# Conv rows stored per weight tile, the sample delta rule by heads, and a later start of the first two delta chunks

## The reference, cut to what matters

```python
h = rmsnorm(x, norm_g)
proj = jnp.einsum('bld,de->ble', h, w_in)
x_ext = jnp.concatenate([conv_prefix, qkv_raw], axis=1)
qkv = causal_short_conv(x_ext, conv_w)          # 4 taps, then SiLU
new_conv = x_ext[:, -(CONV_W - 1):]
o_a, s_new = gated_delta_rule(qa, ka, va, g, beta, s0)       # 4 heads of 128
# per chunk: solve (I + A) against v and k, then
#   v_new = u_c - w_c S ;  o_c = q_c S + attn v_new ;  S = S * gl + k_c^T v_new
o_a = rmsnorm(o_a, dn_norm_g) * silu(z_a)
o_b = merge_dilations(parts) * silu(z_b)        # 8 heads of 64, windows (128,1) (512,4) (2048,16)
y = x + einsum('ble,ed->bld', concatenate([o_a, o_b]), w_out)
y_prompt, y_sample = rmsnorm(yp, final_norm_g), rmsnorm(ys, final_norm_g)
```

## Time and profile before

| | us |
|---|---|
| median of three runs | 1985.62 (1980.72 to 1986.15) |
| the profiled execution | 1983.66 |
| its span in the profile | 1982.0 |
| PE busy in the span | 1726.9 (87%) |

### The profile page before, as it was taken

One profiled execution on the slowest core, in us unless ns is written; L12 is line 12 of the kernel. 1 busy time (PEld: TensorE's weight loads), 2 busy tenths in 40 slices (PEclk: granted clock), 3 DMA queues, 4 the chain that ended last, 5 costly groups with the idle time before them and its releaser, 6 DMA issues. The chain is left out here.

```text
span 1982.0 us, 27674 instructions
## 1 busy us (share of the span) xinstructions
PE 1726.9 (87%) x9674; PEld 1430.6 (72%) x9674; DVE 821.0 (41%) x1890; ACT 639.3 (32%) x1547; POOL 355.2 (18%) x367
## 2 busy tenths in 40 slices
PE   5999999999999998908677898898899559889897
PEld 5998888888888886706577788788788427666674
DVE  3535213511521350154744444444443346445462
ACT  4433212311421230111322443443345214333342
POOL 0000000000000000016023412421422333233231
PEclk9999999999999999958888998898898659999999
DMA  5424586676568679799355547446422456664660
GB/s 173 126 70 156 173 225 170 161 202 225 145 201 204 177 155 127 226 208 280 117 107 147 127 112 181 108 106 171 117 60 70 119 162 197 192 201 154 176 191 32
DMA packets 250186, 309.69 MB, mean 156 GB/s; under 512 B 69244, under 2 KB 198780, under 8 KB 240588
## 3 DMA queue, kind: packets, MB, share of 16 engines
q1 hardware_dynamic: 250068, 308.14, 58.3%
HBM read 228.50 MB, written 146.44 MB: 189 GB/s over the span
## 5 line engine op out<-in xcount | busy, mean ns | idle before, releaser
L326 PE MATMUL pj<-hT_hi,w_hi 128*128 128x512 f32 x896 | 360.1, 402 | 1.8 <-DVE raw L571 1.8
L328 PE MATMUL pj<-hT_hi,w_lo 128*128 128x512 f32 x896 | 352.6, 393 | 0.0
L327 PE MATMUL pj<-hT_lo,w_hi 128*128 128x512 f32 x896 | 352.3, 393 | 0.0
L328 PEld LDWEIGHTS pj<-hT_hi,w_lo 128*128 128x128 f32 x896 | 168.7, 188 | 38.4
L326 PEld LDWEIGHTS pj<-hT_hi,w_hi 128*128 128x128 f32 x896 | 169.0, 189 | 37.0 <-issue 2.1
L327 PEld LDWEIGHTS pj<-hT_lo,w_hi 128*128 128x128 f32 x896 | 169.1, 189 | 34.6
L1477 PE MATMUL o_ps<-pt,vt 128*65 128x256 f32 (+3 forms) x560 | 152.2, 399 | 4.3 <-DVE ot L1699 2.2
L678 POOL IOTA row_at<- 128x1 int32 x1 | 0.1, 139 | 843.3 <-POOLq L2507 843.3
L1541 ACT ACTIVATE pt<-pt_ps 128x512 f32<-128x512 f32 x144 | 84.8, 589 | 157.8 <-PE pt_ps L1455 157.4
L2233 PE MATMUL y_bank<-wo_hi,mh 128*128 128x512 f32 (+1 forms) x272 | 113.2, 416 | 6.8 <-POOL ml L2218 4.6
L533 DVE SCALAR_TENSOR_TENSOR acc<-raw,conv_wt,acc 128x512 f32<-128x512 f32 x144 | 108.3, 752 | 5.1
(11 more groups left out here) (452 smaller groups left out, 3507.3 us busy)
## 6 DMA issues: line engine op xcount, KB each, us to landing
out_dram<-in_cache_k_win_dram SPq DMA_DIRECT2D x56, 584.0 KB, 7.5
out_dram<-in_cache_v_win_dram SPq DMA_DIRECT2D x56, 584.0 KB, 7.0
w_raw<-in_w_in_dram SPq DMA_DIRECT2D x31, 512.0 KB, 10.5
qk_ch<-sil SPq DMA_DIRECT2D x32, 256.0 KB, 3.1
z_ch<-xr SPq DMA_DIRECT2D x32, 256.0 KB, 4.2
wqk<-hi SPq DMA_DIRECT2D x32, 256.0 KB, 5.3
wqk<-lo SPq DMA_DIRECT2D x32, 256.0 KB, 5.3
sc_class<-qk_ch SPq DMA_DIRECT2D x32, 256.0 KB, 4.3
```

The source lines that it names most:

```text
L326: pe.matmul(out, w_hi[s][:, k, :], hT_hi[:, k, cols], start=(k == 0), stop=False)
L327: pe.matmul(out, w_hi[s][:, k, :], hT_lo[:, k, cols], start=False, stop=False)
L328: mm = pe.matmul(out, w_lo[s][:, k, :], hT_hi[:, k, cols], start=False, stop=(k == KT - 1))
```

## The change

It has three parts.

1. Conv rows. SP stores `conv_tail` after each q, k and v tile, one DMA of 128x3 single elements for that tile, 12 in all, in place of three DMAs of 128x12.
2. Opening. `FIRST_DELTA` goes from 9 to 13; the near scores of head 1 keep their places by a new constant `FIRST_NEAR = 9`.
3. Sample. PE turns the sample's own rows before the conv state; DVE makes `linv` and `tab4` later, behind the squares and the first products; POOL makes one weight split, not two, before the inverse roots, and writes `vdb` head by head, and PE's updates wait for their own head; SP stores `k_row` ahead of `linv`, and the state in four DMAs, one per head; DVE's last two weight splits and the output scaling stand among the state updates.

```diff
-                if j == NJ - 1 and kind == "za":
-                    sp.wait_ge(tail_done, 3 * NJ)
+                if kind in ("q", "k", "v"):
+                    at = NJ * y + j
+                    sp.wait_ge(tail_done, 3 * j + y + 1)
                     with nc.allow_non_contiguous_dma(...):
-                        for r in range(TAIL):
-                            sp.dma_start(D.new_conv[r].rearrange("(t p) -> p t", p=P), conv_tail[:, :, r]).then_inc(tail_stored, 16)
+                        sp.dma_start(D.new_conv[:, P * at:P * at + P].rearrange("r p -> p r"), conv_tail[:, at, :]).then_inc(tail_stored, 16)
...
-FIRST_DELTA = 9
+FIRST_NEAR = 9
+FIRST_DELTA = 13
...
-                    if k == (LATEST[q] if q >= 8 else FIRST_DELTA + q // 2 if opening else LATEST[q] + q % 2):
+                    if k == (LATEST[q] if q >= 8 else FIRST_NEAR + q // 2 if opening else LATEST[q] + q % 2):
...
-            sp.wait_ge(G["su_read"], 2 * H)
-            sp.dma_start(D.new_delta_s.rearrange("b h k v -> k b h v"), st[:]).then_inc(G["st_stored"], 16)
+            for h in range(H):
+                sp.wait_ge(G["su_read"], 2 * h + 2)
+                sp.dma_start(D.new_delta_s[:, h].rearrange("b k v -> k b v"), st[:, :, h, :]).then_inc(G["st_stored"], 16)
...
-            split_w(1)
             pool.wait_ge(G["norms"], 1)
...
-            for k in range(2, KT - 2):
+            for k in range(1, KT - 2):
                 split_w(k)
             pool.wait_ge(G["vd"], 1)
-            pool.tensor_tensor(vdb[:], vd4, own, ALU.mult).then_inc(G["vd"], 1)
+            for h in range(H):
+                pool.tensor_tensor(vdb[:, h], svd[:, h].unsqueeze(1).to_broadcast([NS, DEC_BATCH, P]), own, ALU.mult).then_inc(G["vd"], 1)
...
-            pe.wait_ge(G["vd"], 2)
             for h in range(H):
+                pe.wait_ge(G["vd"], 2 + h)
```

## The result

The changed kernel takes 1954.45 us (median of four, 1952.53 to 1957.53), the one before beside it 1985.88: a ratio of 0.985, interval 0.982 to 0.987. So 29 to 31 us are gained, where 39 were forecast. The profiled execution took 1952.53, with a span of 1950.8 (before 1983.66 and 1982.0).

What follows compares the result with a forecast made beforehand. PE, busy 87% of the span, was taken to bound the kernel, with time only where it idles or runs slow. Gains 12.0 + 16.8 + 10.1 = 38.9 us gave 1946; own range 1938 to 1955, wider range 1935 to 1962.

Steps and rivals of the forecast that it cites:

- Conv rows, forecast 12.0: Conv-row stores in `project`: 12.8 us of stall removed, less 0.8 us for twelve small stores, net gain 12.0 us.
- The 12.8 us for the stall: PE at the sample product in `project`: 9.9 us idle plus 2.9 us from a slow stretch, to be removed.
- 4.8 ns each, so one small store keeps them for 1.8 us: Conv-row stores: about 22 us on 4608 elements gives 4.8 ns each, so a 384-element store occupies the DMA engines 1.8 us.
- some 12 us: In `project`, buffers cover some 12 us of an SP stall before PE stands still, so a 1.8 us delay fits.
- small change: Rival: the twelve conv stores cost 0.8 us each, leaving 3 of 12 us gained, time 1955; chance 0.07.
- My own sign for being wrong: For the conv rows in `project`: a landing of a conv store over 8 us.
- the sign for being right: For the conv rows in `project`: no SP issue over some 5 us at a shift.
- Opening, forecast 16.8: Opening of `mixers`: head 1's first delta matmul at 1049.7 against 1066.48, a gain of 16.8 us.
- Sample, forecast 10.1: `sample` phase: 1.4 + 5.3 - 0.8 + 4.2 gives 10.1 us gained, bounds 3 and 14.
- The 1.4 us at `vdb`: In `sample`, POOL reaches `vdb` 1.4 us earlier; bounds a loss of 1.2 and a gain of 3.8.
- 0.8 us: In `sample`, DVE's two weight splits and output scaling among the state updates cost 0.8 us.
- I take 4.0, near the low one, as the others have landed by then: End of `sample`: the last state store, a quarter, is waited for 4.0 us instead of 8.2, gaining 4.2 us.

## Why the prediction was right or wrong

The direction and the range held (1954.45 in 1935 to 1962), and each of the three stalls shrank or went as foreseen. The sum was 7 to 10 us too large, and two terms carry this.

**Conv rows, forecast 12.0, measured 7.0 alone.** The 12.8 us for the stall are right: without small stores `project` ends 12.2 us earlier (846.3 to 834.1). The step that failed is "4.8 ns each, so one small store keeps them for 1.8 us". It took the price per element from three stores that ran together and gave it to one that runs alone. A lone store held SP for 3.5 to 11.4 us in the two kernels counted (changed and conv rows alone). The cover of "some 12 us" was right as a size: in the later tiles such holds cost PE no wait at the sample product, but in the first j two of them, 7 to 11 us, come some 30 us apart, and PE stood still for 0.8 to 7.3 us. So the stores cost 7 to 8 us in the mean, not 0.8. The rival "small change" was nearer (3 of 12 left, measured 4.7 to 7.0) and was given 0.07; that its time, 1955, is the measured one is luck, since `sample` fell short too. My own sign for being wrong was there: conv stores landed after 8.7 us at the least, 9.9 in the median, against a bound of 8; and the sign for being right, no issue over 5 us, failed.

The Trainium skill (DMA: Bandwidth & Descriptors, Anatomy of one DMA) gave the added DMAs an estimated 18 us by its fixed cost of about 2.0 us, a fit for DMAs issued by GpSimd, where these are issued by SP. The runs show 7 to 8 us, and not in that way: one DMA of 512-byte rows costs nothing that shows, and nine more DMAs cost 3.3 us when they stand together (27.7 against 24.4 us). By the same page (Rules for kernel authors) a strided last dimension becomes one descriptor per element, and the trace agrees: in 169 to 182 us of the changed kernel, with one such store of 384 elements, these are the packets:

```profile
DMA packets 834, 0.44 MB, mean 34 GB/s; under 512 B 416, under 2 KB 704, under 8 KB 832
```

**Opening, forecast 16.8, measured 17.4 in this stretch (22 for the part alone).** The steps held: no wait ahead of the first delta matmul, the tile ready 1.7 us before (forecast 2), small waits of the chain 2.1 us in sum (0.27, 0.52, 0.84 and 0.43; forecast 1.6), the end 6.5 us (5.47 and 1.05; forecast 7.1). The spare time is thin: in two of the other seven kernels with this opening PE waited 1.15 and 0.38 us there. Not in the forecast were the 2.4 us at the start of head 2.

**Sample, forecast 10.1, measured 6.0 alone.** PE's updates started 4.3 us earlier against the trace before and 7.4 to 8.1 against the three others of the old form, for a forecast of 6.7 (1.4 and 5.3). The 1.4 us at `vdb` did not come against the trace before: it began 42.5 us into the phase, not 41.7, and no gain there was a sign for being wrong. The reads at the lower clock, 3.1 us longer (13.66 for 10.56), can account for that; against the other three it began 2.3 to 3.0 us earlier. The squares came 2.1 us earlier than in the trace before, not 3.0: POOL's first weight split now lies beside the convolution, and one of its operations took 2.60 us instead of 0.56:

```profile
1537.66 2.60 DVE L2013 TENSOR_TENSOR ctmp<-ext,conv_wt 128x384 f32<-128x384 f32 x1
```

The step that failed is the end, "0.8 us" and "I take 4.0, near the low one, as the others have landed by then". The store's wait is indeed 4.4 us, not 8.2. But from the start of the updates to the end of the phase it is 25.15 us, against 25.4 in the four kernels with one store: 0.3 us gained, not 3.4, and in the other six kernels with this phase it is 25.3 to 26.2, so nothing. DVE's updates end 1.2 us later with the splits among them (16.35 against 15.2 us), and SP reaches the last store late. Its four stores took 11.29 us to issue, the last at 1593.0, and 9.5 us to land in the median: the traffic of 2 MB now stands beside the updates, but its end is hardly earlier.

## What to carry to other kernels

A price per element or per byte that is read from transfers side by side does not hold for one that stands alone. When a stall is to be cut into pieces, look at which pieces fall where buffers are thin, and ask first whether the transfer can be put into long rows: three transposes on an idle bank made the whole cost go. Weigh a gain against more than one profile of the kernel before; here a spell of the clock and a load that landed early hid 3.5 us of it (74.2 against 77.7).

## What the runs showed of the hardware

- 384 single-element writes on their own held the issuing queue for 3.5 to 11.4 us (24 stores in two kernels), with shares of the DMA engines of 0.06 to 1.07 meanwhile; 4608 of them together held it for 24 to 28 us with shares of 0.9 to 1.9.
- DVE operations that take 0.6 to 0.7 us took 2.4 to 2.7 while POOL ran a weight split of 128x1024 (2.4 us), twice in the same phase; the convolution's ended 0.4 us after the split (1540.26 and 1539.85).
- The same 64 matmuls of the state reads took 13.66 us in most profiles and 10.35 or 10.56 in two, at mean clocks of 0.50 and 0.67.
- PE worked for 20 us without a pause at a granted clock of 0.50 in the profile of `FIRST_DELTA = 15`, and for 14 us in the reads of the changed kernel.
